# Where in a body of weight blocks the adaLN weight halves are loaded

## The reference

```python
def adaln_mod(cond, w_mod, b_mod):
    m = jax.nn.silu(cond) @ w_mod + b_mod
    return m.reshape(cond.shape[:-1] + (N_MOD, D_MODEL))      # 9 vectors of 1024

def modulate(x, m, i):
    return x * (1 + m[:, 3 * i + 1][:, None]) + m[:, 3 * i][:, None]

def ffn_sublayer(x, m, i, g, w_in, w_out):
    u = modulate(rms_norm(x, g), m, i)
    return x + 0.5 * m[:, 3 * i + 2][:, None] * swiglu(u, w_in, w_out)
```

## Time and profile before

| | us |
|---|---|
| median of 3 runs | 2788.72 |
| the profiled execution | 2791.35 |
| its span | 2789.5 |
| TensorE busy | 2652.5 (95%) |
| TensorE weight loads | 2282.8 (82%) |
| GpSimd busy | 1364.7 (49%) |
| VectorE busy | 1362.1 (49%) |
| ScalarE busy | 1015.3 (36%) |
| DMA | 365.68 MB, mean 131 GB/s |

### The profile page before, as it was taken

One profiled execution on the slowest core, in us unless ns is written; L12 is line 12 of the kernel. 1 busy time (PEld: TensorE's weight loads), 2 busy tenths in 40 slices (PEclk: granted clock), 3 DMA queues, 4 the chain that ended last, 5 costly groups with the idle time before them and its releaser, 6 DMA issues.

```text
span 2789.5 us, 42914 instructions
## 1 busy us (share of the span) xinstructions
PE 2652.5 (95%) x15048; PEld 2282.8 (82%) x15048; DVE 1362.1 (49%) x2973; ACT 1015.3 (36%) x1651; POOL 1364.7 (49%) x654
## 2 busy tenths in 40 slices
PE   7998989989999999979999999999999999898997
PEld 7968989978888878748887888878888878598997
DVE  3462665575554441482587544454554342616222
ACT  4444457333222232273223322233322132543542
POOL 4606758644444443263443444444444453566875
PEclk9999989989999999999999999999999999999999
DMA  5605635654443442003343443444443442045454
GB/s 189 224 19 166 207 121 185 187 157 139 137 139 113 145 147 87 31 1 121 124 151 120 151 143 117 122 133 145 135 141 113 139 149 76 16 136 167 162 166 124
DMA packets 413993, 365.68 MB, mean 131 GB/s; under 512 B 7484, under 2 KB 412558, under 8 KB 413888
## 3 DMA queue, kind: packets, MB, share of 16 engines
q1 hardware_dynamic: 411448, 359.14, 40.5%
q10 hardware_dynamic: 2440, 5.16, 0.5%
HBM read 363.19 MB, written 1.08 MB: 131 GB/s over the span
## 4 chain that ended last, share of the span: by engine, by line
PE 66%; issue 15%; POOL 13%; DVE 4%; ACT 1%; DMA 0%; POOLq 0%; SPq 0%; DVEq 0%; ACTq 0%
PE bank L1492 56%; POOL w_lo L598 13%; PE bank L1910 1%; PE bank L1552 1%; PE bank L1553 1%; PE bank L1557 1%; DVE stat L1407 1%; PE bank L1888 1%; PE bank L1502 1%; PE bank L1843 1%; PE bank L1644 1%; PE bank L1897 1%; DVE root L1425 1%; PE bank L1835 1%; PE bank L1855 0%
## 5 line engine op out<-in xcount | busy, mean ns | idle before, releaser
L598 POOL TENSOR_TENSOR w_lo<-raw,w_hi 128x1024 fp32r<-128x1024 f32 (+2 forms) x602 | 1285.1, 2149 | 1360.1 <-ACT w_hi L656 987.7
L1492 PE MATMUL bank<-u_hi,w_hi 128*128 128x512 f32 (+1 forms) x2488 | 852.3, 343 | 2.5 <-POOL w_lo L598 2.5
L1492 PE MATMUL bank<-u_hi,w_lo 128*128 128x512 f32 (+1 forms) x2488 | 847.2, 341 | 0.0
L1492 PE MATMUL bank<-u_lo,w_hi 128*128 128x512 f32 (+1 forms) x2488 | 846.6, 340 | 0.0
L656 ACT ACTIVATE w_hi<-raw 128x1024 fp32r<-128x1024 f32 (+3 forms) x436 | 407.2, 951 | 1040.6 <-PE bank L1492 819.9
L1492 PEld LDWEIGHTS bank<-u_hi,w_hi 128*128 128x128 f32 x2488 | 475.1, 191 | 52.7 <-issue 2.7
L1492 PEld LDWEIGHTS bank<-u_hi,w_lo 128*128 128x128 f32 x2488 | 474.9, 191 | 52.3
L1492 PEld LDWEIGHTS bank<-u_lo,w_hi 128*128 128x128 f32 x2488 | 475.3, 191 | 50.1
L1086 DVE SCALAR_TENSOR_TENSOR bank<-mod_raw,cond,bank 128x256 f32<-128x256 f32 x864 | 344.9, 483 | 0.1
L1492 PE MATMUL bank<-hid_hi,w_hi 128*128 128x512 f32 (+1 forms) x880 | 310.2, 352 | 10.9 <-POOL w_lo L598 9.9
L1492 PE MATMUL bank<-hid_lo,w_hi 128*128 128x512 f32 (+1 forms) x880 | 307.4, 349 | 0.0
(11 more groups left out here) (218 smaller groups left out, 3366.2 us busy)
## 6 DMA issues: line engine op xcount, KB each, us to landing
raw<-in_ffn_w_in SPq DMA_DIRECT2D x88, 1024.0 KB, 5.1
mod_raw<-in_w_mod SPq DMA_DIRECT2D x144, 512.0 KB, 3.9
raw<-in_w_in SPq DMA_DIRECT2D x67, 1024.0 KB, 5.1
raw<-in_ffn_w_out SPq DMA_DIRECT2D x64, 704.0 KB, 4.7
raw<-in_w_ffn_up SPq DMA_DIRECT2D x22, 1024.0 KB, 5.1
raw<-in_w_ffn_down SPq DMA_DIRECT2D x16, 704.0 KB, 4.8
raw<-in_w_attn_out SPq DMA_DIRECT2D x8, 1024.0 KB, 5.2
raw<-in_w_o SPq DMA_DIRECT2D x8, 1024.0 KB, 5.5
```

Of the source, the lines that this page charges most:

```text
L598: pool.tensor_tensor(st.half(t, w_lo[slot]), st.half(t, raw[slot]), st.half(t, w_hi[slot]).bitcast(f32), ALU.subtract).then_inc(lo_ready, 1)
L1492: ins = pe.matmul(dst, s, v, start=first and n == 0, stop=final and n == 2)
```

## The change

In SP's `body` the two halves of a body's adaLN pair are issued behind the load of the body's first block, no longer behind that of its last. What each load waits for is as before, and so is everything on the other engines.

```diff
                     load(st, i, c)
-                    if st.mod and c == st.per - 1:
+                    if st.mod and c == 0:
                         mod_loads(st, i)
```

## The result

| | before | after |
|---|---|---|
| median of 5 runs each | 2791.91 us | 2801.54 us (2800.99 to 2802.06) |
| the profiled execution | 2791.35 us | 2801.12 us |
| its span | 2789.5 us | 2799.3 us |

The changed kernel is slower: ratio 1.0040, 95% interval 1.0026 to 1.0055, so 11 us (7 to 15); the ratio compares all executions, whose means differ by 11.3 us, while the medians differ by 9.6. The forecast was 2803.0.

The account below looks back on a forecast made before the run. TensorE, busy 95% of the span, bounds the kernel, so little can be won. 5.2 (`qk_mb`) + (2.9 + 1.7) (`gates1_1`) + (3.8 + 1.7) (`q_1`) - 1.0 (`down1`) = 14.3 us on 2788.72 gives 2803.0; range 2794 to 2812.

Parts of the forecast that it names:

- The three places: `qk_mb` second body, `gates1_1` first body, `q_1` last block: late weight blocks make TensorE wait 3.5, 2.9 and 3.8 us.
- clock, forecast: Behind each new TensorE wait the granted clock falls to 0.50, costing 1.7 us each; bounds 0 and twice that.
- two small lags: `gates1_1`: halves delaying block 27 (0.2 us) and late block 30 holding up ScalarE's gates (0.6) add 0.8 us.
- ScalarE's chain of split, table load and `lam_e`: `qk_mb`: late block 9 makes this chain 4.1 us late; TensorE's own path, 5.2 us late, overtakes it.
- `down1`: Four-block bodies with early products: a gain of 1.0 us in all, -0.5 for the bodies and 0.5 at the end.
- the loop of load and split: `down1` bodies: the `raw` slot's loop sets their 19 us in either order, so -0.5 us, bounds -3 and +1.
- For the end I had 0.5 us: End of `down1`: sums some 5 us sooner, but block 82 late, so the root at 589.5 against 589.99.
- the 18.5 that the prediction names as a sign of being wrong: A `down1` body under 18.5 us would show the prediction wrong.
- The wide bodies: 512-column bodies: 0 us, as second blocks have cover, 13 us in `up_01` and at least 6 in layer 0's others.
- (a): Blocks late but TensorE feels little, through cover, no clock fall or `down1` payback: 2788 to 2797 us, chance 0.24.
- (b): Faster: removing VectorE's waits reaches TensorE in `down1`, bodies 3.4 and end 5 us, price 8.4: 2780.3 us, chance 0.03.
- (c): Much slower: wide cover is less than read, 33 up bodies each lose 0.5 us and more: from 2819, chance 0.05.

Follow-up runs that it names:

- e11: Kernel before, with halves behind the first of four blocks in `down1` alone: 2785.12 us, ratio 0.9984.
- e10: Kernel before, with halves behind the first block only in two-block 512-column Gemms other than the three up products: ratio 1.0000.
- e12: Kernel before, with halves behind the first block only in the 30 later bodies of the three up products: ratio 0.9999.
- e3: Kernel before, with halves behind the first block only in the two-block Gemms with 512 columns: 2794.30 us, ratio 1.0018.
- e9: Kernel before, with halves behind the first block in `up_00`, `up_01` and `up_10` alone: ratio 1.0017.
- e8: Kernel before, with the first half of each pair behind the first block and the second behind the last: ratio 1.0016.
- e4: Kernel before, with SP's product waits and 16-byte loads behind the first block of two-block bodies, halves still behind the last: 2808.05 us, ratio 1.0063.

## Why the prediction was right, step by step

**The three places** were the right ones, for the reason given, and no other arose. What was forecast and what came:

| place | wait, forecast | wait, after | clock, forecast | clock, after | sum |
|---|---|---|---|---|---|
| `qk_mb` | 3.5 | 3.3 | 1.7 | 2.7 | 5.2 / 6.0 |
| `gates1_1` | 2.9 | 3.9 | 1.7 | 1.4 | 4.6 / 5.3 |
| `q_1` | 3.8 | 3.9 | 1.7 | 1.5 | 5.5 / 5.4 |

(The gaps of the last two rows are those between starts of matmuls.) Block 7 was to go out at 72.1 and be ready at 81.6; it went at 71.93 and was ready at 81.6. The wait of `gates1_1` was sized too low. SP's rows of after show why.

```profile
285.60 3.49 SPq L550 DMA_DIRECT2D mod_raw<-in_w_mod  x2
289.14 1.13 SPq L541 DMA_DIRECT2D raw<-in_w_in  x2
```

The halves of pair 7 went out at 285.60, which less the lag of 4.6 us is 281.0, against 279.42 before: the products were 1.6 us late, where I had put down 0.8 for two small lags. In `q_1` there is no such lag, and the wait came out to a tenth of a microsecond.

**`qk_mb` behind the wait.** I let ScalarE's chain of split, table load and `lam_e` be 4.1 us late and TensorE's path 5.2, so that TensorE's decides. So it was: `lam_e` came at 94.59, 6.3 us later than in rows 6, for TensorE's matmuls ran 6.0 us late. The lag then fell to 4.8 by 105 us, mostly because the stretch at the lower clock that stood at 90 to 97 us before (89.95 to 96.8) was shorter after (97.6 to 101.0).

**`down1` was the term that was mis-sized**: -1.0 forecast, -4.5 measured alone. Two steps of that term failed. For the bodies I held that the loop of load and split sets their 19 us, so that an earlier product is worth next to nothing; but the waits of TensorE for the products (3.4 us) went away and came back as time for the most part, 2.8 us in e11. Its bodies take 18.9, 18.3 and 18.3 us (19.5, 19.0 and 18.9 before), two of them under the 18.5 that the prediction names as a sign of being wrong; after the change they are 19.25, 18.54 and 18.59. For the end I had 0.5 us: block 82 late, the root at the same distance but a little shorter. Block 82 was late as forecast, and the root came right behind its split and table load, as forecast; ScalarE of after:

```profile
592.54 2.00 ACT L645 ACTIVATE w_hi<-raw 128x1024 fp32r<-128x1024 f32 x2 [3.89 <-DMA raw<-in_ffn_w_in]
594.56 1.28 ACT L723 ACT_TABLE_LOAD   x1
595.86 0.26 ACT L723 ACTIVATE rms<-bank,eps 128x2 f32<-128x2 f32 x1
```

The way from `modulate` to L1654 took 7.15 us instead of 8.28, 1.1 won, twice the forecast. Alone (e11) it takes 6.42: in the changed kernel the halves of `up_00` also stand ahead of block 82 and cost 0.7 of it.

**The wide bodies** cost nothing, as said; e10 and e12 show it by themselves. What the prediction didn't have is that the first body of `up_00` costs 2.2 us where `down1` is not changed too (e3, e9). In the whole change this is hidden, and in a telling way: with early halves in `down1` its last products are done sooner, so the halves of `up_00` don't have to wait for them. SP of after, with block 81, the halves of `up_00` and block 82:

```profile
581.45 0.38 SPq L541 DMA_DIRECT2D raw<-in_ffn_w_in  x1
581.88 1.12 SPq L550 DMA_DIRECT2D mod_raw<-in_w_mod  x2
586.70 6.50 SPq L541 DMA_DIRECT2D raw<-in_ffn_w_in  x2
```

**The sum.** Forecast +14.3. In the two traces the lag is 0.3 ahead of the first place, and the three places add 16.7 us. 1.7 are gone between 90 and 272 us. From 308 to 591 us the lag falls by 4.1: 1.1 of it at 382 us, behind the norm, where a stretch at the lower clock is shorter, and 2.9 from just ahead of the first `modulate` of `down1` (524.86 before) to L1654. Another 1.3 lie between 591 and 2257 us, in pieces of 0.4. It ends at 9.8. The ratio gives 11 (7 to 15), the medians 9.6, the single experiments add up to 13.7 - 4.5 = 9.2 for the narrow Gemms and `down1`. So the forecast was 2 to 3.5 us high for `down1` and 1.4 low for the places, and it had no term for the 4 us that came back between the places, mostly where stretches at the lower clock are shorter than before. That the time of 2803.0 lies only 1.5 from 2801.5 is partly luck: it starts from a median of three runs, and that of five is 3.2 us higher. The upper end of the range is not worked out either: its terms end at 2808.6, and "a little more for landings" stands for 3.4 us.

**The rivals.** (a) "Late but little felt" fell: all three places were felt in full where they arise. A part of it was true, `down1` paid back 3 to 5 us. (b) Its mechanism is real, but gave 4.5 of its 8.4 us, and the places cost three times that. (c) fell with e10 and e12.

The Trainium skill (DMA: Bandwidth & Descriptors, "Rules for kernel authors") advises to issue early and wait late. Where that was all that happened, in `down1`, the runs agree: 4.5 us won (4.7 in the trace, up to L1654). In the narrow bodies the early issue carried a wait ahead of the next load, and there it cost 5 to 6 us a place.

## What to carry over

In a queue that runs in order, a DMA with a wait of its own is priced by what stands behind it: before moving it forward, list the loads it is moved past, and for each the time at which its user wants it. A load that was 13 us early can be made late by a step that itself gains something. Move such a step only in those stages where its wait is already over at the new position (here the four-block bodies of `down1`: 4.5 us faster), and look at the first body behind a stage change by itself, since what stands there is also ahead of the norm. A wait of an engine that isn't the bottleneck (122.8 us of VectorE) says nothing of what removing it is worth.

## What the runs showed of the hardware beyond the forecast

- What a late block costs isn't proportional to its lateness. With TensorE idle for 3.3 to 3.9 us the granted clock went to 0.50 in each of the three places and added 1.4 to 2.7 us; with 0.7 us idle, at two of the same places, it stayed at 1.00 and added nothing (e8). So in `q_1` 3.7 us idle cost 5.4, and 0.7 idle cost 0.9. Between these the length doesn't decide: in e4 2.5 us idle at the gates were followed by 3.4 us at 0.50, and 2.6 us idle in `q_1` by none.
- The same place can fall on either side without an edit. At the end of `gates1_1`, which is as before in e3, TensorE's pause is longer in e3's execution than in before's, 1.50 us and no fall there; the windows of e3:

```profile
325.60:328.30 2.70, 0.32 (x3) 0.11 (x1) 2.17 (x7) 2.27 (x3) 1.80 (x2) 0.98 0.23 44
328.30:331.60 3.30, 3.29 (x15) 3.29 (x16) 2.63 (x7) 0.00 (x0) 3.30 (x2) 0.50 0.82 281
```

  With the longer pause that is 2.7 us, as much as the whole effect of some edits here. And ahead of the first place, at 71.7 us, the other traces lie from 3.8 us before to 0.3 us behind the one of before. A difference in the traces has to be looked up where it arises before it is laid to an edit.
- A 1 MB load behind one or two halves took 6.2 and 6.3 us from issue to landing (block 7 in after and in e8), whether one half (68.03) or two (68.39 and 71.5) were ahead of it: with two, the first had landed by then. With none ahead, in e4, it took 5.5.
- A VectorE operation that starts while GpSimd splits a block can take several times as long. In e4, ahead of the norm behind `w_o_0`, VectorE's last sum and last square (L1073 and L1068, 128x512) started 0.2 and 0.3 us behind the start of a split, took 2.77 and 2.59 us and ended 0.5 us behind the split's end; in before the same two took 0.69 each, having started with GpSimd idle. A weight block that TensorE doesn't wait for can cost time in this way.
